# A two-layer decoder step on one core: in the softmax attention, projections and the samples' work moved on by one iteration

## The reference, cut to what matters

```
q = (a @ p['w_q_b'][j]).reshape(B, L, ATT_KV_HEADS, ATT_GROUP, ATT_HEAD_DIM)
s = jnp.einsum('bqngd,bknd->bngqk', q, k) * ATT_HEAD_DIM ** -0.5 + bias
m = jnp.maximum(jnp.max(s, axis=-1, keepdims=True), sink)
p = jnp.exp(s - m)
denom = jnp.sum(p, axis=-1, keepdims=True) + jnp.exp(sink - m)
o = jnp.einsum('bngqk,bknd->bqngd', (p / denom), v)
m = o @ p['w_o_b'][j]
```

## Time and profile before

| | |
|---|---|
| three runs | 2792.39, 2798.29, 2800.5 us; median 2798.29 us |
| the profiled execution | 2794.6 us |
| its span, first to last instruction | 2792.8 us |
| mean granted TensorE clock | 0.955 of full speed |
| PE, DVE, ACT, POOL busy | 90%, 59%, 41%, 3% of the span |
| the attention loop | `scores(0)` starts at 1495.8 us, `downs(7)` at 1933.1 us |

### The profile page before, as it was taken

The page is one execution under the profiler, slowest core; times in us unless marked ns, Lnnn a source line. Parts: engine busy times, 40 slices in busy tenths (PEclk is TensorE's granted clock), DMA queues, the critical chain, the costliest instruction groups (busy, mean ns, idle before and its releaser), DMA issues.

```text
span 2792.8 us, 37637 instructions
## 1 busy us (share of the span) xinstructions
PE 2521.1 (90%) x15437; PEld 2206.9 (79%) x15437; DVE 1654.8 (59%) x2811; ACT 1140.4 (41%) x1792; POOL 85.5 (3%) x22
## 2 busy tenths in 40 slices
PE   2999999998999999999997889878999999999994
PEld 1777888887778879999995666667777888999994
DVE  2677556665665555765555666665665555655554
ACT  2555444343443324333334656553443333333232
POOL 0000000000010000010000110000001000000000
PEclk8999999988999999999998899989999999999997
DMA  7222213322422323323223222221332232332222
GB/s 153 78 67 76 84 63 101 106 85 81 155 78 96 98 76 96 133 74 99 84 84 100 74 90 76 67 93 34 107 129 91 93 98 79 106 118 80 88 91 75
DMA packets 93799, 255.17 MB, mean 91 GB/s; under 512 B 10947, under 2 KB 44204, under 8 KB 91820
## 3 DMA queue, kind: packets, MB, share of 16 engines
q1 hardware_dynamic: 69916, 209.24, 24.1%
q10 hardware_dynamic: 23712, 43.52, 4.4%
HBM read 225.92 MB, written 26.74 MB: 90 GB/s over the span
## 4 chain that ended last, share of the span: by engine, by line
PE 39%; DVE 5%; ACT 4%; issue 3%; DMA 1%; POOL 1%; ACTq 0%; DVEq 0%
PE banks L431 23%; PE banks L451 13%; DMA normed<-h_scratch 1%; ACT w_hi L409 1%; DVE w_lo L414 1%; PE banks L1569 1%; PE banks L1543 1%; ACT probs L1860 1%; PE banks L1555 1%; POOL act_lo L574 1%; DVE normed L561 0%; ACT act_hi L570 0%; DVE hf L1371 0%; DVE stats L1724 0%; ACT normed L488 0%
## 5 line engine op out<-in xcount | busy, mean ns | idle before, releaser
L431 PE MATMUL banks<-act_hi,w_lo 128*128 128x272 f32 (+1 forms) x2952 | 977.1, 331 | 49.5 <-DVE act_lo L574 21.1
L431 PE MATMUL banks<-act_hi,w_hi 128*128 128x272 f32 (+1 forms) x2952 | 963.1, 326 | 0.0
L431 PE MATMUL banks<-act_lo,w_hi 128*128 128x272 f32 (+1 forms) x2952 | 961.8, 326 | 0.0
L409 ACT ACTIVATE w_hi<-w_raw 128x1024 fp32r<-128x1024 f32 x366 | 380.5, 1055 | 778.8 <-PE banks L451 518.4
L414 DVE TENSOR_TENSOR w_lo<-w_raw,w_hi 128x1024 fp32r<-128x1024 f32 x366 | 464.8, 1283 | 375.9 <-ACT w_hi L409 375.7
L431 PEld LDWEIGHTS banks<-act_hi,w_lo 128*128 128x128 f32 x2952 | 562.5, 191 | 112.9 <-issue 27.4
L431 PEld LDWEIGHTS banks<-act_lo,w_hi 128*128 128x128 f32 x2952 | 563.5, 191 | 44.0 <-issue 1.7
L431 PEld LDWEIGHTS banks<-act_hi,w_hi 128*128 128x128 f32 x2952 | 561.7, 190 | 44.0
L463 DVE TENSOR_TENSOR acc<-acc,banks 128x272 f32<-128x272 f32 (+1 forms) x624 | 315.9, 518 | 216.5 <-PE banks L451 212.5
L451 PE MATMUL banks<-h_hi,w_lo 128*128 128x272 f32 (+1 forms) x1056 | 354.9, 336 | 59.0 <-issue 36.1
L451 PE MATMUL banks<-h_lo,w_hi 128*128 128x272 f32 (+1 forms) x1056 | 351.4, 333 | 0.0
(11 more groups left out here) (209 smaller groups left out, 2657.8 us busy)
## 6 DMA issues: line engine op xcount, KB each, us to landing
w_raw<-wall SPq DMA_DIRECT2D x366, 512.0 KB, 3.6
normed<-h_scratch ACTq DMA_DIRECT2D x12, 704.0 KB, 4.7
h_scratch<-acc ACTq DMA_DIRECT2D x3, 2176.0 KB, 8.5
h_scratch<-acc ACTq DMA_DIRECT2D x3, 2048.0 KB, 8.3
gstates<-state ACTq DMA_DIRECT2D x4, 1024.0 KB, 6.2
gla_s<-gstates ACTq DMA_DIRECT2D x4, 1024.0 KB, 4.0
bias<-bias_scratch SPq DMA_DIRECT2D x32, 128.0 KB, 3.6
bias_scratch<-bias_rows SPq DMA_DIRECT2D x1, 3064.0 KB, 36.6
```

The lines of the kernel that those rows point to most:

```text
L409: nc.scalar.activation(WH[:, b % RING], WR[:, b % RAW], ACT.Copy).then_inc(w_hi, 1)
L431: last = nc.tensor.matmul(PS[:, bank, 0:n], w, a[X][:, k, o:o + n], start=(k == 0 and first), stop=(k == KT - 1 and w is wh and a is AH))
```

## The change

In the loop, round and place in the round are now taken from s - 1, and the loop has one more turn. So every projection, the weights' roundings for them, the second halves' third norm and the samples' work come one s later, while `scores`, `biased`, `exps` and the rest of the 64 iterations stay. The first pass of norms stays at its s, the second is moved on by one. `s_new` is put at w = 3 on PE and at the head of w = 4 on DVE, so it stays at its s; DVE did it after the adds, and now does it before `divided`.

```
-                  40: 0, 42: 1, 47: 2, 49: 3, 51: 4, 53: 5, 55: 6, 57: 7, 59: 8}
+                  41: 0, 43: 1, 48: 2, 50: 3, 52: 4, 54: 5, 56: 6, 58: 7, 60: 8}
...
-        PE_AT = {3: 2, 11: 6, 47: 2, 55: 6}
-        SUM_BANK = {3: 6, 11: 6, 47: 5, 55: 5}
+        PE_AT = {3: 2, 11: 6, 48: 2, 56: 6}
+        SUM_BANK = {3: 6, 11: 6, 48: 5, 56: 5}
...
-            for s in range(NIT + 4):
-                k, w = divmod(s, 8)
+            for s in range(NIT + 5):
+                k, w = divmod(s - 1, 8)
...
-                if d >= 0 and w == 4 and d < 4:
+                if d >= 0 and w == 3 and d < 4:
                     s_new(d)
...
-                if s in (20, 22):
-                    by_token((s - 20) // 2)
+                if s in (21, 23):
+                    by_token((s - 21) // 2)
...
+                if d >= 0 and w == 4:
+                    s_new(d)
                 if 1 <= s <= NIT:
                     divided(s - 1)
...
                     elif w == 5:
-                        s_new(d)
                         s_add(d, 0)
...
-                if s in (18, 21):
-                    dve_norm(dve, 2, "mix", 1, (s - 18) // 3)
+                if s in (19, 22):
+                    dve_norm(dve, 2, "mix", 1, (s - 19) // 3)
...
-                elif w == 7 and k:
+                elif w == 7 and k > 0:
                     downs_done(k - 1)
...
-                if s in (20, 22):
-                    act_hi(act, 2, "mix", 1, (s - 20) // 2)
+                if s in (21, 23):
+                    act_hi(act, 2, "mix", 1, (s - 21) // 2)
```

More of the change, by code:

```diff
@@ L1502, in build @@
         ACT_AT = {0: 0, 1: 1, 3: 2, 5: 3, 7: 4, 9: 5, 11: 6, 13: 7, 15: 8,
-                  40: 0, 42: 1, 47: 2, 49: 3, 51: 4, 53: 5, 55: 6, 57: 7, 59: 8}
+                  41: 0, 43: 1, 48: 2, 50: 3, 52: 4, 54: 5, 56: 6, 58: 7, 60: 8}
         DVE_AT = {1: (0,), 2: (1,), 4: (2, (0,)), 5: (2, (1,)), 6: (3,), 8: (4,), 10: (5,), 12: (6,), 14: (7,),
-                  41: (0,), 43: (1,), 48: (2, (0,)), 49: (2, (1,)), 50: (3, (0,)), 51: (3, (1,)), 52: (4,), 54: (5,), 56: (6,), 58: (7,)}
-        PE_AT = {3: 2, 11: 6, 47: 2, 55: 6}
-        SUM_BANK = {3: 6, 11: 6, 47: 5, 55: 5}
+                  42: (0,), 44: (1,), 49: (2, (0,)), 50: (2, (1,)), 51: (3, (0,)), 52: (3, (1,)), 53: (4,), 55: (5,), 57: (6,), 59: (7,)}
+        PE_AT = {3: 2, 11: 6, 48: 2, 56: 6}
+        SUM_BANK = {3: 6, 11: 6, 48: 5, 56: 5}
         def pass_at(s):
@@ L1696, in pe_att @@
                 if s in PE_AT:
-                    if s >= 47:
+                    if s >= 48:
                         pe.wait_ge(xsa, 3 * d + 3)
```

## The result

The changed kernel takes 2812.87 us (median of 5 runs, 2810.76 to 2815.66), the kernel before 2798.51 in the 5 runs beside them: a ratio of 1.0052, 95% interval 1.0040 to 1.0063. That is 14.4 us more, slower by more than 0.3%, and outside the predicted range of 2789 to 2805. The profiled execution has a span of 2811.1 us and a mean granted clock of 0.951.

The account below looks back on a forecast made before the run. PE was taken as bound by its own work where projections lie between attention iterations, elsewhere by DVE stuck in norm steps. Terms -0.1 - 0.4 + 0.9 + 3.2 - 2.0 - 0.5 - 2.0 = -0.9 us gave 2797.4; 8-in-10 range 2789 to 2805.

Parts of the forecast that it names:

- the delays by parity: `lo` now at even w, delaying DVE's work: +4.0 us at w = 4 of round 2, +3.2 at w = 0, rounds 5 to 7.
- the slower rival: `lo` at w = 0 and w = 4 wholly on the path: 10.7 us over the sum, 2808 us; chance 13%.
- Parity: `lo` leaves the quarters at w = 7 (-0.4 three times), comes before the adds at w = 4 (+0.4 twice): -0.4 us.
- Start, -0.1: From the loop's start to round 2: gains on the norm chain are owed for work that is now later, -0.1 us.
- the chain over POOL: At the start, from `biased(13)` through exps, high part, POOL and second normed half to `lo`, ending at 1582.3 against 1587.5.
- Round 2, +0.9: At w = 4 `lo` delays a weight block's rest, +4.0 us; a later wait for `biased(21)` goes, -3.1: +0.9.
- wait of PE over 5 us: Sign of being wrong: PE waiting over 5 us at a place the prediction did not list.
- w = 0 in rounds 5 to 7, +3.2: `lo` now stands before two rests and `s_scaled`, delaying PE's `s_transposed`: +1.8, +0.2 and +1.2 us.
- the places of round 7 without a projection (-2.0): Near s = 59 DVE's wait for POOL comes after `lo`, so `values(56)` and `scores(60)` go through: -2.0 us.
- the samples' add (-0.5): PE's waits at the samples' first add, 3.1 us in 4: only 0.1 us each of 0.7 to 1.0 won, -0.5.
- The sinks' copy caught by POOL: Rival: in the first pass POOL's second subtraction holds the sinks' copy at iterations 16 and 17: +3.4 us, 2801; chance 12%.
- End, -2.0: From s = 63 to `downs(7)`: a wait, `scores` and earlier transposes and values go, `lo(61)` adds 2.0: -2.0 us in all.

Follow-up runs that it names:

- `lo` behind in round 2 only: The changed kernel with `lo` put behind `biased` and the weight blocks' rests in round 2 alone, `s_new` left alone: 2807.24 us, ratio 1.0035.
- the rests first: The changed kernel with the weight blocks' rests at the head of their s, before `lo` and `biased`, `lo` still before `biased`: 2800.47 us, ratio 1.0004.

## Why the prediction was wrong, point by point

The mechanism was on record, as the delays by parity and as the slower rival. The places and the sizes were not. The prediction's sum was -0.9; the runs gave +14.4, and the loop of the traced pair +17.7. Three terms failed, all for the same reason, that `lo` at the head of an s was priced at some of the places where it now stands: round 2, the quarters at w = 4 of rounds 5 and 6 (under "Parity"), and round 7. The steps, each measured at the same place:

- **Start, -0.1: +1.0 came.** The sum holds, its last part only by luck. `scores(1)` came 2.79 us after the first (2.8 forecast), the wait for the copy of queries was 1.46 instead of 2.2, and the normed values started 69.1 us after the first `scores` (69.5 forecast). But `values(12)` at 1582.07 only seems to meet the forecast of 1582.3: this trace's loop starts 2.2 us earlier, so it came 2.0 later. Nor did it wait for `lo`, as the chain over POOL had it. PE was held earlier by DVE's adds (1.67 and 2.47 us), the second time by adds behind a negation that took 4.68 us beside POOL's subtraction:

```profile
1496.37 0.76 PE L1543 MATMUL banks<-kg,q 64*128 64x256 f32 x4 [2.30 <-DVE scores L1719]
...
1507.52 0.47 PE L431 MATMUL banks<-act_hi,w_lo 128*128 128x512 f32 x1 [1.46 <-ACT q L1851]
...
1577.66 0.47 PE L451 MATMUL banks<-o_hi,w_lo 128*128 128x512 f32 x1 [2.47 <-DVE acc L461]
...
1582.07 0.49 PE L1569 MATMUL banks<-probs_t,v_tok 128*64 128x128 f32 x4
```

- **Round 2, +0.9: +7.5 came.** This is the first step that failed. Its own two terms were right: the quarter at w = 4 cost +3.3 (+4.0 forecast), and -3.8 came back behind it (-3.1 forecast). What it left out is w = 0 and w = 2, where the same `lo` now stands before the same pair of rests: +2.3 and +4.3 by the starts of `scores`; another +1.6 in w = 6 and 7 is not traced further. The prediction had named the rule ("all of DVE stands behind it, and PE's `scores` behind that") and priced it at one of three places of the round. With `lo` behind in round 2 only, k3 w0 stands at +0.9, so in these traces `lo`'s place is all of it.
- **Parity, -0.4: the adds at w = 4, "+0.4 twice", are the second step that failed.** It counted the 0.42 us that `lo` takes and not the wait and the work between: in round 6 the quarter lost +3.4, with PE waiting 6.43 us. (In round 5 it lost nothing, -0.5.) Such a wait of PE over 5 us at none of its places is the sign of being wrong that the prediction had named, and so is the one of 5.87 in round 7.
- **w = 0 in rounds 5 to 7, +3.2.** PE's waits for L1783 in those three rounds are 4.24, 1.86 and 1.76, so 7.9, against 2.37 before: +5.5 gross, where a wait of 4 us at s = 41 had been foretold and came. With the places of round 7 without a projection (-2.0) and the samples' add (-0.5) the forecast from k5 w0 to k7 w4 was +0.7; +4.3 came. The wait for L1752 did turn into one for L1758 and gave 0.7. Rounds 3 and 4 gave -2.8 that no step foresaw.
- **The sinks' copy caught by POOL** was a rival at 12%, +3.4, put in iterations 16 and 17. There the copy beside POOL's second subtraction took 0.31, so next to nothing came. (With `lo` behind in round 2 only, the copy of iteration 17 was held for 3.30 us, and still `scores` at k2 w1 stood at +3.0, against +3.2 in the changed kernel.) It came at s = 61, in a step of 7.6 us, and this is the third step that failed: "places without a projection" looked at the wait that goes (s = 59) and not at what DVE does when POOL's second half starts. It is not left to timing, as the rival had it: `hi` follows the high part on ACT, so `lo`, and the copy behind it, start 0.2 and 0.7 us after POOL: the copy at 1904.13 behind 1903.39 in the changed kernel, and at 1893.29 behind 1892.54 with the rests first, which is 0.74 and 0.75, though the two traces are 11 us apart by then. In the five traces with `lo` behind `biased` there, the copy took 0.14 or 0.15.
- **End, -2.0: +0.3 came.** The wait before the samples' transposes did fall, but one of 3.18 for ACT's transposed probabilities stands in front of it, and PE works at the lower clock level behind (0.50).

The slower rival (2808) had the right cause and was still 5 us short, because it counted the same few places; one of its terms, that round 2's +3.1 is not given back, did not come (-3.8 did). Against it the prediction held that DVE is idle long in the waits that follow. In the table something is taken back in rounds 3 and 4 (-2.8) and in w = 5 of round 2 (-3.8), but the column of the changed kernel never returns to its +1.0. The price of a waiting instruction at the head of an in-order queue is not its own wait: DVE waited 44 us longer for `hi` (86.2 less 42.2) where the kernel lost 14.4, and in the kernel before the same wait fell by 33 us and nothing was gained.

Two pages bear on it. The Trainium skill ("PSUM — Partial Sum Buffer", Engine vs sequencer instructions) says that VectorE's queue is strictly first in, first out. The trace agrees: for 9.49 us in round 2 nothing behind `lo` started, though the rounded block of the first rest had been ready since 1628.4. And the Trainium skill ("SBUF — State Buffer", Who interferes with whom) says that whoever is second at the port pair that DVE and GpSimd share is fully blocked, while a VectorE operation with at most one input in SBUF, outside the two-port modes, is not. The trace agrees in both halves: the copy from SBUF ended when POOL did (3.80 us), and `lo`, with one input in PSUM, took 0.43 inside the same subtraction.

The best kernel of the case is the changed one with `lo` and `s_new` behind `biased` and the rests: 2793.19 us, 0.9987 [0.9976, 0.9998] of the kernel before, 5.2 us by the medians and 3.6 by the ratio.

## What to carry to other kernels

When a change shifts work against instructions that come only every second turn, list every place where the pair now meets, with what stands behind it, and price them all; one place worked out well says little about the sum. On an in-order engine, try an instruction that waits for another engine behind the work that is ready and that the bound engine asks for next; in the kernel before, the same move gave nothing on balance. Where two instructions are released by the same engine within a fraction of a microsecond, look at what the engines they start will share.

## What was not expected of the hardware

POOL's subtraction held a copy of 128 x 2 elements for 3.80 us, and in the first pass a negation of 128 x 2 for 4.68 us, while `lo`, with an input in PSUM, ran at its usual length inside the same stretch, as did a reciprocal of 128 x 2 from SBUF (0.16 us at 1904.06). The line of the negation in the changed kernel:

```profile
1572.24 4.68 DVE L1726 TENSOR_SCALAR stats<-stats 128x2 f32<-128x2 f32 x1
```

So in this case a DVE instruction's size did not decide whether it was held. And a gap of PE cost more than its length: after one of 5.87 us, the granted clock was 0.56 for the next 4 us, and the same matmul took 0.43 instead of 0.29.
